# A two-block transformer kernel on one core: pool tiles in two buffers, another bank order in w_out's first row and in the last values, and the last three rows finished half by half

## The reference

```
# pool mixer, group g of 128 channels, window w
lo, hi = max(t - w//2, 0), min(t + w//2 - 1, L - 1)
diff = (csum[hi+1] - csum[lo]) / (hi - lo + 1) - x
y = (diff @ w_pool[g] + b_pool[g]) * scale
# first block
x = x + concat([y_a, y_b, y_c]) @ w_out
x = x + (silu(gate) * val) @ ffn_w_down ; x = rmsnorm(x)
# second block
x = x + rmsnorm_2(fox_attention(rmsnorm_2(x)), g1)
h = square(relu(rmsnorm_2(x) @ w1)) @ w2
out = x + rmsnorm_2(h, g3)          # the root is over the 2048 columns of a token
```

## Time and profile before

| | |
|---|---|
| Median of 3 runs | 2201.43 us (2201.28 to 2202.84) |
| The profiled execution | 2201.5 us, its span 2199.7 us |
| Granted TensorE clock, mean | 0.998 of 2.4 GHz |
| TensorE (PE) busy | 2166.7 us, 99% |
| VectorE (DVE) busy | 1312.5 us, 60% |
| ScalarE (ACT) busy | 1009.4 us, 46% |
| DMA | 410.30 MB, mean 187 GB/s |

### The profile page before, as it was taken

One profiled execution on the slowest core, in us unless ns is written; L12 is line 12 of the kernel. 1 busy time (PEld: TensorE's weight loads), 2 busy tenths in 40 slices (PEclk: granted clock), 3 DMA queues, 4 the chain that ended last, 5 costly groups with the idle time before them and its releaser, 6 DMA issues.

```text
span 2199.7 us, 27911 instructions
## 1 busy us (share of the span) xinstructions
PE 2166.7 (99%) x11682; PEld 1860.2 (85%) x11682; DVE 1312.5 (60%) x1612; ACT 1009.4 (46%) x1181; POOL 51.2 (2%) x76
## 2 busy tenths in 40 slices
PE   7999999999999999999999999999999999999998
PEld 6788888888888888888898889878888888888886
DVE  7967547777676775444655565456555555444444
ACT  5444436555555544333554444445333334433333
POOL 1030000000000000000001010000000000000000
PEclk9999999999999999999999999999999999999999
DMA  9554655655555555555566555546666665555552
GB/s 311 161 177 156 210 186 178 201 182 192 192 191 192 191 188 185 187 189 189 156 217 195 170 173 186 188 129 215 187 189 189 192 191 191 188 186 187 189 190 95
DMA packets 267949, 410.30 MB, mean 187 GB/s; under 512 B 6645, under 2 KB 246325, under 8 KB 249392
## 3 DMA queue, kind: packets, MB, share of 16 engines
q1 hardware_dynamic: 264672, 395.47, 54.9%
q0 software_dynamic: 2432, 11.74, 1.5%
q10 hardware_dynamic: 720, 1.31, 0.2%
HBM read 406.38 MB, written 2.11 MB: 186 GB/s over the span
## 4 chain that ended last, share of the span: by engine, by line
PE 93%; DVE 3%; ACT 1%; issue 1%; DMA 1%; DVEq 0%; SPq 0%; ACTq 0%
PE bank L1382 33%; PE bank L1395 17%; PE bank L1419 11%; PE bank L1424 11%; PE bank L1420 11%; PE bank L1385 2%; PE bank L1386 2%; PE bank L1397 2%; DMA raw<-in_w_in 1%; ACT whi L405 1%; DVE wlo L692 1%; PE bank L1276 1%; PE bank L1230 0%; DVE M L1166 0%; PE bank L1363 0%
## 5 line engine op out<-in xcount | busy, mean ns | idle before, releaser
L692 DVE TENSOR_TENSOR wlo<-raw,whi 128x2048 fp32r<-128x2048 f32 (+1 forms) x374 | 857.2, 2293 | 790.7 <-ACT whi L405 790.7
L405 ACT ACTIVATE whi<-raw 128x2048 fp32r<-128x2048 f32 (+1 forms) x374 | 716.5, 1918 | 800.2 <-PE bank L1424 438.6
L1382 PE MATMUL bank<-hh,whi 128*128 128x512 f32 x3392 | 826.1, 396 | 16.6 <-ACT whi L405 10.9
L1382 PEld LDWEIGHTS bank<-hh,whi 128*128 128x128 f32 x3392 | 626.9, 189 | 148.5 <-ACT whi L405 10.9
L1395 PEld LDWEIGHTS bank<-hh,wlo 128*128 128x128 f32 x3392 | 429.7, 188 | 17.6 <-DVE wlo L692 0.4
L1395 PE MATMUL bank<-hh,wlo 128*128 128x256 f32 x3392 | 434.9, 281 | 0.0
L1419 PE MATMUL bank<-whi,hh 128*128 128x512 f32 x1088 | 428.8, 394 | 2.2 <-DVE M L855 2.2
L1420 PE MATMUL bank<-whi,hh 128*128 128x512 f32 x1088 | 427.5, 393 | 0.0
L1424 PE MATMUL bank<-wlo,hh 128*128 128x512 f32 x1088 | 274.3, 394 | 0.0
L1419 PEld LDWEIGHTS bank<-whi,hh 128*128 128x128 f32 x1088 | 204.5, 188 | 50.8 <-issue 2.4
L1424 PEld LDWEIGHTS bank<-wlo,hh 128*128 128x128 f32 x1088 | 204.3, 188 | 47.4
(11 more groups left out here) (225 smaller groups left out, 864.3 us busy)
## 6 DMA issues: line engine op xcount, KB each, us to landing
raw<-in_mlp_w SPq DMA_DIRECT2D x128, 1024.0 KB, 5.5
raw<-in_ffn_w_up SPq DMA_DIRECT2D x88, 1024.0 KB, 5.1
raw<-in_ffn_w_down SPq DMA_DIRECT2D x44, 1024.0 KB, 4.8
raw<-in_w_in SPq DMA_DIRECT2D x34, 1024.0 KB, 5.5
raw<-in_fox_w_in SPq DMA_DIRECT2D x32, 1024.0 KB, 5.3
raw<-in_fox_w_in SPq DMA_DIRECT2D x16, 1032.0 KB, 5.4
raw<-in_w_out SPq DMA_DIRECT2D x16, 1024.0 KB, 4.9
raw<-in_fox_w_out SPq DMA_DIRECT2D x16, 1024.0 KB, 4.7
```

Source lines behind the costliest of these rows:

```text
L405: e.activation(whi[i % RING][:, 0:n], raw[i % RAW][:, 0:n], ACT.Copy).then_inc(s_hi, 1)
L692: e.tensor_tensor(wlo[i % RING][:, 0:n], raw[i % RAW][:, 0:n], whi[i % RING][:, 0:n].bitcast(F), ALU.subtract).then_inc(s_lo, 1)
L1382: e.matmul(bank[b][:, :], wh[:, k, s], hh[:, kk, :], start=kk == 0, stop=False)
```

## The change

Pool: the two tiles of a group are copied and added first, into `pp[:, 0]` and `pp[:, 3]`; `pool_out(n)` holds both additions, with a semaphore `s_pe` of their own for which units 28 and 30 wait. The window sums follow, tile by tile. In `SIDE`, entry 28 and 29 name the pool work ahead of the pool_mix. `w_out`'s first row takes the columns in the order 3, 1, 2, 0 in place of 0, 1, 3, 2. Values 9 to 15 all run behind unit 229, in that order.

The last projection: its rows stage stops three rows early, and `last_rows` does the last three rows. For half 0 all four banks are finished, then half 1 bank by bank, nine matmuls each. The root is taken for each half: three of the four column parts are summed beforehand (`three_chunks`), and the last one goes into ScalarE's root with the rest as bias. `mlp_r` computes the epsilon term `v_2` ahead, with two more VectorE operations. The results of half 0 stand between the gain multiplications of half 1. The last result (columns 3 of half 1) is made by TensorE: identity times the residual plus a diagonal of the root times the product, two plain float32 matmuls of 512 columns, copied out and sent by ScalarE. SyncE issues the other seven output DMAs.

```diff
-    27: [("pool", 0), ("pool", 1)], 28: [("pool_mix", 0), ("pool", 2)], 29: [("pool_mix", 1), ("pool", 3)],
+    27: [("pool", 0), ("pool2", 1)], 28: [("pool", 2), ("pool_mix", 0)], 29: [("pool2", 3), ("pool_mix", 1)],
-    194: [("sums", 0)], 228: [("early", 2), ("values", 8)], 229: [("values", 9), ("values", 10)],
+    194: [("sums", 0)], 228: [("early", 2), ("values", 8)],
-LAST_VALUES = (11, 15, 12, 13, 14)
-VALUES_ORDER = (*range(8), 8, 9, 10, *LAST_VALUES)
+LAST_VALUES = range(9, NH)
+POOLED = (0, 5, 11, 18, 26)
+VALUES_V = (*[10] * 8, 12, 12, 14, 14, 16, 16, 16, 14)
-ROWS = ((U_OUT, KD, (0, 1, 3, 2)), ...
+ROWS = ((U_OUT, KD, (3, 1, 2, 0)), ...
+QS_LAST = [(j, h) for h in range(2) for j in range(4)]
# SyncE
-            for q in range(0, 8, 2):
-                j, h = QS[q]
+            for q, (j, h) in enumerate(QS_LAST[:7]):
                 e.wait_ge(s_fd, q + 1)
                 e.dma_start(out[:, h, 512 * j:512 * j + 512], Xt[:, h, 512 * j:512 * j + 512]).then_inc(s_outd, 16)
# ScalarE
                         if n:
-                            e.wait_ge(s_pg, (0, 6, 13, 21)[n])
-                        small_terms(n, pp[:, 0, 16:16 + T]).then_inc(s_pgs, 1)
+                            e.wait_ge(s_pg, POOLED[n])
+                        for m in (0, 1):
+                            small_terms(n + m, pp[:, 3 * m, 16:16 + T]).then_inc(s_pgs, 1)
-            for q, (j, h) in enumerate(QS):
+            for q, (j, h) in enumerate(QS_LAST):
                 e.wait_ge(*row_done(3, q))
-                square_sum(5, q, bank[BANKS[j][h]][:, :], 4 * h + j)
-            root(8, r_t)
+                square_sum(5, q, bank[BANKS[j][h]][:, :], q)
+                if j == 3:
+                    e.wait_ge(s_ss, SS0[5] + q + 1)
+                    e.wait_ge(s_part, 2 * h + 2)
+                    e.activation(r_t[:, h:h + 1], SS[5][:, q:q + 1], ACT.Sqrt, bias=part[:, h:h + 1], scale=1.0 / D).then_inc(s_root, 1)
+            x = Xt[:, 1, 1536:D]
+            e.wait_ge(s_ty, 1)
+            e.activation(x, bank[BANKS[0][0]][:, :], ACT.Copy).then_inc(s_tx, 1)
+            e.wait_ge(s_tx, 1)
+            e.dma_start(out[:, 1, 1536:D], x).then_inc(s_outp, 16)
# VectorE
+            def pool_out(n):
+                e.wait_ge(s_unit, U_IN + 2 * (12 + n // 2) + 2)
+                for m in (0, 1):
+                    a0 = pp[:, 3 * m, 16:16 + T]
+                    e.wait_ge(s_pgs, n + m + 1)
+                    e.tensor_tensor(a0, bank[n + m][:, 0:T], a0, ALU.add).then_inc(s_pe, 1)
-                        e.tensor_tensor(r_4, r_2, r_2, ALU.mult).then_inc(s_rr, 1)
+                        e.tensor_tensor(v_2, r_2, r_2, ALU.mult).then_inc(s_rr, 1)
+                        e.wait_ge(s_rr, 5)
+                        e.reciprocal(v_2, v_2).then_inc(s_rr, 1)
+                        e.wait_ge(s_rr, 6)
+                        e.tensor_scalar(v_2, v_2, RMS_EPS, None, ALU.mult).then_inc(s_rr, 1)
+            for q in range(3):
+                gained(5, q, ytail, g3r)
+            three_chunks(0)
+            gained(5, 3, ytail, g3r)
+            last_root(0)
+            for q in range(3):
+                gained(5, 4 + q, ytail, g3r)
+                result(q)
+            three_chunks(1)
+            result(3)
+            gained(5, 7, ytail, g3r)
+            last_root(1)
+            e.tensor_scalar(dg[:, 0, :], ident[:, :], r_t[:, 1:2], None, ALU.mult).then_inc(s_dg, 1)
+            for q in range(4, 7):
+                result(q)
# TensorE
+                for j in range(4):
+                    three(n - 3, j, 0)
+                three(n - 2, 0, 0)
+                three(n - 2, 1, 0)
+                three(n - 1, 0, 0, True)
+                three(n - 1, 1, 0, True)
+                for j in (2, 3):
+                    three(n - 2, j, 0)
+                    three(n - 1, j, 0, True)
+                for j in range(4):
+                    three(n - 3, j, 1)
+                    three(n - 2, j, 1)
+                    three(n - 1, j, 1, True)
+                o = bank[BANKS[0][0]][:, :]
+                e.wait_ge(s_yg, 8 + 1)
+                e.matmul(o, ident[:, :], Xt[:, 1, 1536:D], start=True, stop=False)
+                e.wait_ge(s_yg, 8 + 8)
+                e.wait_ge(s_dg, 5)
+                e.matmul(o, dg[:, 0, :], ytail[:, 1, 1536:D], start=False, stop=True).then_inc(s_ty, 1)
```

More of the change, by code:

```diff
@@ L225, in two_block_program @@
         gx = view(0, 4096, 2, D)
-        r_up, r_a, r_aq, r_b, r_y, r_2, r_4, r_t = (st[:, 64 + 2 * n:66 + 2 * n] for n in range(8))
+        r_up, r_a, r_aq, r_b, r_y, r_2, v_2, r_t = (st[:, 64 + 2 * n:66 + 2 * n] for n in range(8))
         s_raw = [sem(f"s_raw{i}") for i in range(RAW)]
@@ L1016, in side @@
                     elif what == "pool":
+                        pool_out(n)
+                        pool_group(n)
+                    elif what == "pool2":
                         pool_group(n)
@@ L1200, in vector, with three_chunks, last_root, result @@
             rows(3)
[L1202 to L1213, removed]
+            def three_chunks(h):
+                p = part[:, h:h + 1]
+                e.wait_ge(s_ss, SS0[5] + 4 * h + 3)
+                e.tensor_reduce(p, SS[5][:, 4 * h:4 * h + 3], AX.X, ALU.add).then_inc(s_part, 1)
+                e.wait_ge(s_part, 2 * h + 1)
+                e.scalar_tensor_tensor(p, p, 1.0 / D, v_2[:, h:h + 1], ALU.mult, ALU.add).then_inc(s_part, 1)
+            def last_root(h):
+                e.wait_ge(s_root, 8 + h)
+                e.reciprocal(r_t[:, h:h + 1], r_t[:, h:h + 1]).then_inc(s_rcp, 1)
+                e.wait_ge(s_rcp, 8 + h)
+            def result(q):
+                j, h = QS_LAST[q]
                 x = Xt[:, h, 512 * j:512 * j + 512]
@@ L1408, in rows @@
                 u0, n, order = ROWS[stage]
-                for k in range(n):
+                for k in range(n if stage < 3 else n - 3):
                     u, s = u0 + k, row_slot(stage, k)
@@ L1436, in rows, with last_rows, three @@
                             turn(stage, j - 2)
+            def last_rows():
+                def three(k, j, h, done=False):
+                    u, s, c, o, tok = U_W2 + k, row_slot(3, k), slice(512 * j, 512 * j + 512), bank[BANKS[j][h]][:, :], slice(h * P, h * P + P)
+                    e.matmul(o, hhi[:, s, tok], whi[u % RING][:, c], start=False, stop=False)
+                    e.matmul(o, hlo[:, s, tok], whi[u % RING][:, c], start=False, stop=False)
+                    e.wait_ge(s_lo, u + 1)
+                    t = e.matmul(o, hhi[:, s, tok], wlo[u % RING][:, c], start=False, stop=done)
+                    if done:
+                        t.then_inc(s_row, 1)
+                n = FF2 // P
+                e.wait_ge(s_hi, NU - 2)
+                e.wait_ge(s_alo, ROW0[3] + n - 2)
+                for j in range(4):
+                    three(n - 3, j, 0)
+                e.wait_ge(s_hi, NU - 1)
+                e.wait_ge(s_alo, ROW0[3] + n - 1)
+                three(n - 2, 0, 0)
+                three(n - 2, 1, 0)
+                e.wait_ge(s_hi, NU)
+                e.wait_ge(s_alo, ROW0[3] + n)
+                three(n - 1, 0, 0, True)
[13 more added lines that the diff above has]
+                e.matmul(o, dg[:, 0, :], ytail[:, 1, 1536:D], start=False, stop=True).then_inc(s_ty, 1)
             def in_free(g, n):
@@ L1491, in tensor @@
                 values(h)
-            rows(2, [(s_v, 15), (s_v, 16), (s_v, 13), (s_v, 14), *[(s_pvt, VALUES_ORDER.index(h) + 1) for h in (12, 13, 14, 15)]])
+            rows(2, [(s_v, 15), (s_v, 16), (s_v, 13), (s_v, 14), *[(s_pvt, h + 1) for h in (12, 13, 14, 15)]])
             e.wait_ge(s_yg, 1)
```

53 lines of the change are left out of this document (23 added, 30 removed).

## The result

The changed kernel takes 2192.72 us (median of 5 executions, 2189.57 to 2194.58) against 2201.43 us (5 executions, 2201.22 to 2204.55): a ratio of 0.9954, 95% interval 0.9941 to 0.9968, faster by 0.46%. The forecast was 2189.7 with a range of 2188.2 to 2193.6. The time is in the range, 3.0 us above the forecast.

What follows compares the result with a forecast made beforehand. TensorE, busy 2166.7 of 2199.7 us, was taken as the bound, so only its waits, low clock and the end count. Gains 4.74 + 2.68 + 1.16 + 3.1 = 11.7 us off 2201.4 give 2189.7, range 2188.2 to 2193.6.

Steps and rivals of the forecast that it cites:

- A: Unit 28 waiting for the pool tiles: 3.69 us to gain, about 2.0 of it the wait and 1.67 the low clock.
- B: Third and fourth pool tile, at unit 30: 1.05 us to gain, from the same cause as at unit 28.
- C: w_out's first row waiting for banks 4 and 5: 2.68 us to gain, with no clock part.
- D: The seven values after unit 229, value 15 waiting for 11's copy: 1.16 us to gain, bounds 0.8 and 1.16.
- The last rows: Last three rows of the last projection: 72 matmuls stay 72 at 0.234 us; 0 to 0.3 us lost, taken as 0.
- the last low part: Last rows: ready at 2176.89, the first matmul needing it starting near 2177.0; tight, 0 to 0.3 us lost, taken as 0.
- The sum over A to D: Pool tiles, w_out's first row and values together: the last matmul of the rows about 8.6 us earlier.
- E: From the last matmul to the span's end, 10.5 us before: gain 3.1 us, bounds 2.4 and 3.7.
- VectorE's order behind the last matmul: After the last matmul at 2189.17: result 3 from about 2189.6, eighth multiplication to 2190.96, reciprocal to 2191.14.
- The DMA part of the step: Last output DMAs: four pieces from 2192.14 end at 2196.7, the last issue alone gives 2196.0; 2196.6 taken.
- the rival that had 8%: A clock fall of the same length comes elsewhere than at unit 28: 1.7 us lost, 2191.4; chance 8%.
- allowances for the clock, the pool and the end: Upper end of the range, 2193.6: 1.7 us of clock, 1.5 at the pool and 0.7 at the end.

Runs made afterwards that it cites:

- the runs that took something from the first piece: Changed kernel with eight unused matmuls at 84 us: three quarters of half 1's first output DMA left out, 2189.51 us; that result made and sent in two pieces, 2189.66 us.
- the later groups: The kernel before, unaltered, timed again beside each group of follow-up runs: medians 2203.10, 2203.05 and 2202.79 us.
- the values part: Only the new order of the values (9 to 15 behind unit 229), on the kernel before with eight unused matmuls at 84 us: median 2199.55 us, lowest 2198.38.
- the kernel before, filled at 84 us: Eight matmuls with unused results put into TensorE's idle stretch at 84 us of the kernel before: median 2199.84 us, 2199.41 to 2202.45.
- filled at A as well: Kernel before with eight unused matmuls at 84 us and eight more ahead of unit 28, its wait left as is: 2200.71 us, 2199.57 to 2201.33.
- the run of the end alone: Only the last rows and the end as in the change, on the kernel before with eight unused matmuls at 84 us: median 2197.44 us, lowest 2195.89.

## Why the prediction was right, point by point

**A and B.** The mechanism was right: additions first, no gap at unit 28, none at unit 30, no consumer late behind VectorE. Of the 4.74 us, 3.1 are the waits and were measured as such (3.07 by the lowest times, 3.08 by the traces). The other 1.67, the clock at A, was a price of one execution and not of the kernel; its size was nearly right (1.59).

**C and D.** Right: 2.68 in the traces (2.55 by the lowest times) for 2.68, and 1.13 (1.03) for 1.16.

**The last rows.** Nothing to speak of was lost at the last low part. From w_out's first row to the last matmul the two profiles differ by 1.08 us, D's 1.14 less 0.06. The sum over A to D came out at 8.5 us in the profiles, as predicted (8.6), with A's fall of the clock counted in both.

**E.** The gain is 3.5 us, not 3.1. The step that was mis-sized is VectorE's order behind the last matmul: result 3 began 0.20 us after the last matmul's end, not 0.44, and the reciprocal 1.46 us after, not 1.79. The DMA part of the step gave a good number by a wrong picture: the sum over four pieces and the one over the last two agree to 0.1 us, and the runs that took something from the first piece show that it doesn't count. The rule of the Trainium skill that was cited there ("DMA: Bandwidth & Descriptors", "Issuing engines are not separate DMA queues") is that DMAs of different issuing engines share the 16 DMA engines. It holds: the DMA sent by ScalarE and the last of SyncE's, 0.1 us apart, landed after 2.5 and 2.7 us instead of 2.1.

**What was missing, 3.0 us.** This is the rival that had 8%: the clock falls all the same. Its price was too low (1.7 us; at 84 us it is 3.4), and so was its chance: by the times it happened in eight of ten executions. The step that failed is the sum's use of one profiled execution: it counted a fall seen once at A as a cost of A, and doesn't mention the 2.17 us of idle time at 84 us, behind which the clock had stayed up in that trace. The kernel before has four places behind which a fall was seen; the change removes two of them and leaves the ones at 50 and 84 us. Against the kernel before as timed in the later groups (2203.1) the changed kernel gains 10.4 us, which is the 10.26 us of waits and end: each of the two medians holds some 3.2 us of falls, and these cancel. The median of 2201.43 was that of five executions, three of which had the smallest loss that this kernel shows.

**What was luck.** The forecast of 2189.7 is within 0.2 us of the changed kernel's time without falls (2189.52), but only since the fall in the 2201.43 was taken off again as a gain at A. The measured median lies in the range because its upper end adds up allowances for the clock, the pool and the end (1.7, 1.5 and 0.7 us): the pool and the end lost nothing, and the clock alone took more than its own 1.7. With the later groups' 2203.1 as the time before, the same sum would give 2191.4.

**A version that beats both.** The changed kernel with the stretch at 84 us filled takes 2189.52 us, and 2189.38 without TensorE's last piece: ratio 0.9937 to the kernel before, interval 0.9924 to 0.9949. Against the changed kernel's ten executions (median 2192.67) that is 3.3 us less, and the scatter shrinks from 5 to 0.1 us in five executions.

## What to carry to other kernels

Find what a unit waits for by name, bank by bank: if the last reader of a bank sits behind work that TensorE doesn't need, move the read ahead, give it its own buffer, or take the banks in the order in which they come free. Here such gains added up and could be summed from the chain of waits to within a few tenths of a microsecond. Price a low clock from several executions, never from one trace: here idle stretches of 1.4 to 2.2 us cost 1.6 to 3.4 us more behind them or nothing, and a few unused matmuls in them told which. In the kernel before, filling one stretch of four did not end the scatter; filling all four did. At the end of a kernel ask which of the last transfers wait for each other before an engine's work is moved to gain an earlier issue.

## What the runs showed of the hardware

Falls of the granted clock to 0.50 (1.2 GHz) were seen behind four idle stretches of TensorE, and each of the four was also seen with the clock left at 1.00:

| idle stretch | fall in the trace of | none in the trace of |
|---|---|---|
| at 50 us, 1.4 us | the values part (1.41) | the kernel before (1.42) |
| at 84 us, 2.1 to 2.2 us | the changed kernel (2.14) | the kernel before (2.17) |
| at A, 1.8 us | the kernel before (1.80) | the kernel before, filled at 84 us (1.80) |
| at C, 2.2 us | filled at A as well (2.19) | the kernel before (2.19) |

So the length of the stretch doesn't tell whether the clock falls. Each time the falls lasted about 3.4 us, or 6.8 us at 84 us, where four plain float32 matmuls of 384 columns come first. Of the six falls in the traces five began 0.7 to 1.3 us after TensorE was at work again (at 87.3 us where work resumed at 86.6), and one, at C in the run of the end alone, just as work resumed (241.8 and 241.9). In no execution without the filling did the kernel before escape a fall, judged by its times (lowest 2201.05 in all groups, against 2199.4 with the one stretch at 84 us filled). I had not expected that and cannot explain it from these runs: where a fall at 84 us is absent, another one seems to be there. "TensorE: Matmul & The Clock Gate" of the Trainium skill, Part 1, says that the watch runs free of the kernel's start. The executions agree with it in that one and the same kernel loses 3.2 us in one and nothing in another (2192.7 and 2189.5 us).
